# A fifth quad by seven products in gate/up pairs 1 to 8, with nine low parts a pair on GpSimd

## The reference

```python
    h = rmsnorm(x, norm_ffn[l])
    x = x + (jax.nn.silu(h @ w_gate[l]) * (h @ w_up[l])) @ w_down[l]
```

## Time and profile before

| | us |
|---|---|
| median of 3 runs | 2156.8 |
| lowest and highest of them | 2156.14 to 2157.34 |
| span of the profiled execution | 2155.3 |
| TensorE matmuls busy in it | 2144.2 |
| VectorE busy | 1771.7 |
| ScalarE busy | 1218.7 |
| GpSimd busy | 314.5 |

### The profile page before, as it was taken

One profiled execution on the slowest core, in us unless ns is written; L12 is line 12 of the kernel. 1 busy time (PEld: TensorE's weight loads), 2 busy tenths in 40 slices (PEclk: granted clock), 3 DMA queues, 4 the chain that ended last, 5 costly groups with the idle time before them and its releaser, 6 DMA issues.

```text
span 2155.3 us, 27924 instructions
## 1 busy us (share of the span) xinstructions
PE 2144.2 (99%) x10397; PEld 1794.4 (83%) x10397; DVE 1771.7 (82%) x2143; ACT 1218.7 (57%) x1714; POOL 314.5 (15%) x310
## 2 busy tenths in 40 slices
PE   9999999999999999999999999999999999999998
PEld 7888888888888888888888888888888888888886
DVE  5776676899899988999866666768998998988997
ACT  6454455666566555556554555546665665655564
POOL 0031120211221110000001211201112112100010
PEclk9999999999999999999999999999999999999999
DMA  9654445777777776767766444557777777756685
GB/s 349 203 183 176 176 157 189 212 218 223 246 217 229 227 229 205 227 216 221 246 200 217 171 161 157 176 194 212 218 229 232 219 222 244 221 198 219 219 240 181
DMA packets 152872, 456.81 MB, mean 212 GB/s; under 512 B 17440, under 2 KB 18080, under 8 KB 152352
## 3 DMA queue, kind: packets, MB, share of 16 engines
q1 hardware_dynamic: 132624, 416.41, 55.5%
q0 software_dynamic: 18816, 35.66, 9.8%
q10 hardware_dynamic: 1296, 2.94, 0.4%
HBM read 448.65 MB, written 2.10 MB: 209 GB/s over the span
## 4 chain that ended last, share of the span: by engine, by line
PE 97%; DVE 1%; ACT 1%; DMA 1%; POOL 0%; issue 0%; ACTq 0%; SPq 0%; DVEq 0%
PE bank L1861 16%; PE bank L1863 16%; PE bank L1862 16%; PE bank L1835 14%; PE bank L1875 9%; PE bank L1874 9%; PE bank L1873 9%; PE bank L1838 7%; PE bank L2039 1%; PE bank L1998 1%; PE bank L2021 1%; PE bank L1977 0%; DMA raw<-w_gu_dram 0%; POOL o_rms L675 0%; DVE wlo L1191 0%; PE bank L2007 0%
## 5 line engine op out<-in xcount | busy, mean ns | idle before, releaser
L761 ACT ACTIVATE whi<-raw 128x1024 fp32r<-128x1024 f32 x540 | 553.9, 1056 | 195.2 <-PE bank L1863 137.4
L1184 DVE TENSOR_TENSOR wlo<-raw,whi 128x1024 fp32r<-128x1024 f32 x504 | 606.9, 1229 | 65.9 <-ACT whi L761 64.9
L767 ACT ACTIVATE whi<-raw 128x1024 fp32r<-128x1024 f32 x480 | 430.0, 944 | 241.7 <-DVE raw L1206 139.6
L1191 DVE TENSOR_TENSOR wlo<-raw,whi 128x1024 fp32r<-128x1024 f32 x480 | 501.0, 1084 | 49.7 <-ACT whi L767 46.4
L1835 PE MATMUL bank<-xg,whi 128*128 128x512 f32 x1280 | 406.9, 399 | 1.0 <-DVE wlo L1440 1.0
L1861 PE MATMUL bank<-whi,xg 128*128 128x512 f32 x864 | 339.3, 393 | 0.5 <-DVE wlo L1184 0.5
L1863 PE MATMUL bank<-whi,xg 128*128 128x512 f32 x864 | 336.7, 390 | 0.0
L1862 PE MATMUL bank<-wlo,xg 128*128 128x512 f32 x864 | 336.5, 389 | 0.0
L1838 PEld LDWEIGHTS bank<-xg,wlo 128*128 128x128 f32 x1280 | 240.5, 188 | 56.9
L1838 PE MATMUL bank<-xg,wlo 128*128 128x256 f32 x1280 | 252.0, 278 | 0.0
L1835 PEld LDWEIGHTS bank<-xg,whi 128*128 128x128 f32 x1280 | 195.0, 189 | 3.3 <-DVE xg L1434 1.4
(11 more groups left out here) (161 smaller groups left out, 3050.7 us busy)
## 6 DMA issues: line engine op xcount, KB each, us to landing
raw<-w_gu_dram SPq DMA_DIRECT2D x268, 512.0 KB, 4.9
raw<-w_in_dram SPq DMA_DIRECT2D x188, 512.0 KB, 4.5
raw<-w_down_dram SPq DMA_DIRECT2D x140, 512.0 KB, 5.4
raw<-w_gu_dram SPq DMA_DIRECT2D x168, 256.0 KB, 4.2
raw<-w_out_dram SPq DMA_DIRECT2D x64, 512.0 KB, 4.4
raw<-w_gu_dram POOLq DMA_DIRECT2D x84, 256.0 KB, 5.7
raw<-w_down_dram SPq DMA_DIRECT2D x72, 256.0 KB, 4.7
raw<-w_down_dram POOLq DMA_DIRECT2D x36, 256.0 KB, 6.1
```

Source lines behind the costliest of these rows:

```text
L761: act.activation(whi[:, blk.slot(k)], raw[:, slot, half * UNIT_KT:(half + 1) * UNIT_KT, :], ACT.Copy).then_inc(hi_ready, 1)
L767: act.activation(whi[:, quad.slot(n), 0:tiles.stop - tiles.start], raw[:, quad.raw(), tiles, :], ACT.Copy).then_inc(hi_ready, 1)
L1184: dve.tensor_tensor(wlo[:, blk.slot(k)], raw[:, slot, half * UNIT_KT:(half + 1) * UNIT_KT, :], lo_bits(whi[:, blk.slot(k)]), ALU.subtract) ...
L1191: dve.tensor_tensor(wlo[:, quad.slot(n), into], raw[:, quad.raw(), tiles, :], lo_bits(whi[:, quad.slot(n), into]), ALU.subtract).then_inc( ...
```

## The change

- `GU_SEVENS` goes from 4 to 5: pairs 1 to 8 (`GU_FIVES`) do units 0 to 4 as quads and units 5 to 7 plainly, in a new order (`gu_five` on each engine). Pair 9 keeps four quads. Pair 0 does too, and in it the token-side forms of the fifth quad are made, by VectorE and ScalarE.
- In these eight pairs GpSimd makes nine low parts: of both units 5, both units 6 and the right unit 7, and the last part (two tiles) of quads 0 to 3. VectorE keeps the low parts of left unit 7, all first parts, the other second parts and all sums. In pair 0 GpSimd makes three low parts (right 5, left 6, right 7). It has no wait for a sum copy ahead of these.
- The three tiles of a quad's first parts are split by one operation on ScalarE and one on VectorE instead of two each, in every gate/up pair but the last.
- The high and low parts lie in ten tiles, placed by lists (`GU_FIVE_TILES` and others) instead of five slots in turn.
- Two more places for raw weights lie where `resid` is. ScalarE stores `resid` to DRAM in pair 0 (waiting for its squares), SP waits for the store ahead of pair 1's loads, loads it back ahead of pair 10's, and VectorE's fold of the first down pair waits for it.
- `sum_out` of a pair moves on ScalarE from its end to behind the first unit of the next pair.

```diff
-NSPLIT = 5
+NRAW_GU = NRAW + 2
+SPLIT_TILES = 10
...
-GU_SEVENS = 4
+GU_SEVENS = 5
...
-GU_FOURS = range(1, NGU // 2 - 1)
+GU_FIVE_ORDER = [("left", 5), ("right", 5), ("first", 0), ("first", 1), ("left", 6), ("second", 0), ("first", 2),
+                 ("right", 6), ("second", 1), ("first", 3), ("second", 2), ("first", 4), ("second", 3), ("second", 4),
+                 ("left", 7), ("right", 7)]
+GU_FIVE_TILES = [8, 6, 3, 0, 8, 6, 3, 0, 8, 5, 3, 0, 8, 6, 3, 0, 8, 6, 2, 4, 0]
+GU_FIVES = range(1, NGU // 2 - 2)
+GU_FOUR = NGU // 2 - 2
...
+    raw_gu = at("raw_gu", [P, NRAW_GU - NRAW, LOAD_KT, COLS], F32, resid_at)
+    resid_kept = nc.dram_tensor("resid_kept", (DEPTH, P, QT, DM), F32, kind="Internal").ap()
...
             for blk in plan.blocks[2:]:
+                if isinstance(blk, Pair) and blk.name == "gu" and blk.i == GU_FIVES[0]:
+                    sp.wait_ge(resid_out, 16 * (blk.layer + 1))
...
+                    sp.dma_start(resid[:], resid_kept[blk.layer]).then_inc(resid_back, 16)
...
+                for p in GU_FIVES:
+                    pair, later = (plan.pairs[layer, "gu", n] for n in (p, p + 1))
+                    left, right = pair.blocks
+                    split(left, 5)
+                    split(right, 5)
+                    add_b(pair.quads[2])
+                    split(left, 6)
+                    split_last(pair.quads[0])
+                    add_b(pair.quads[3])
+                    split(right, 6)
+                    split_last(pair.quads[1])
+                    add_b(pair.quads[4])
+                    split_last(pair.quads[2])
+                    split_last(pair.quads[3])
+                    add_b(later.quads[0])
+                    if later.five:
+                        add_b(later.quads[1])
+                    split(right, 7)
...
+                act.wait_ge(squared, (ffn + 1) * QT * NCH)
+                act.dma_start(resid_kept[layer], resid[:]).then_inc(resid_out, 16)
...
+            def gu_five(pair, prior):
+
+                q = [pair.quads[k] for k in range(GU_SEVENS)]
+                layer, before = prior.layer, [b.i for b in prior.blocks]
+                gates_ups(prior, 0, 1)
+                gates_ups(prior, 1, 0)
+                gates_ups(prior, 1, 1)
+                hidden_products(layer, before[0], 0)
+                hidden_products(layer, before[0], 1)
+                first_parts(q[0])
+                hidden_products(layer, before[1], 0)
+                hidden_products(layer, before[1], 1)
+                hidden_low(layer, before[0])
+                first_parts(q[1])
+                sums_of(q[0])
+                hidden_low(layer, before[1])
+                second_part(q[0])
+                sums_of(q[1])
+                first_parts(q[2])
+                second_part(q[1])
+                sums_of(q[2])
+                first_parts(q[3])
+                second_part(q[2])
+                sums_of(q[3])
+                first_parts(q[4])
+                sums_of(q[4])
+                second_part(q[3])
+                second_parts(q[4])
+                split(pair.blocks[0], 7, 8)
+                gu_fold(pair)
+                gates_ups(pair, 0, 0)
```

More of the change, by code:

```diff
@@ L196, in __init__ @@
                 q.added = plan.places[q.raw()]
-            if part in ("first", "second"):
+                q.joint = self.five or self.fours
+                q.split = [plan.split_unit(q.loads, t) for t in ((3,) if q.joint else (2, 1))]
+            elif part == "second":
                 q = self.quads[k]
-                q.split += [plan.split_unit(q.loads), plan.split_unit(q.loads)]
+                q.split += [plan.split_unit(q.loads, 2), plan.split_unit(q.loads, 2, by_pool=self.five and k in POOL_SECONDS)]
             else:
-                plan.unit(blocks[part == "right"], k, by_pool=self.fours and not self.first and k == POOL_UNIT)
+                plan.unit(blocks[part == "right"], k, by_pool=self.five and (part, k) != ("left", 7) or self.first and (part, k) in POOL_FIRST
+                          or self.fours and not self.first and k == POOL_UNIT)
         self.sums_taken = plan.taken[max(q.split[-1] for q in self.quads.values())][1]
@@ L268, in __init__, with split_unit @@
                         self.blocks.append(pair)
[L270 removed]
+    def split_unit(self, loads, tiles, block=None, last=False, by_pool=False):
         if last:
@@ L276, in split_unit @@
         n = len(self.taken) - 1
+        taken = tiles + tiles % 2 if tiles < 3 else tiles
+        if self.given:
+            self.next_tile = self.given.pop(0)
+        elif self.next_tile + taken > SPLIT_TILES:
+            self.next_tile = 0
+        span = slice(self.next_tile, self.next_tile + tiles)
+        self.span.append(span)
+        self.next_tile += taken
+        held = max(self.tile_held[span])
+        self.after.append(held if held >= 0 else None)
+        self.tile_held[span] = [n] * tiles
         for load in loads:
-            load.last = n
+            load.last["pool" if by_pool else "dve"] = n
         if by_pool:
@@ L918, in gu_rest @@
                 second_parts(q2)
+                if pair.first:
+                    form_high(pair.layer, "gu", GU_BATCHES - 1)
                 split(right, 6, 7)
@@ L1329, in gu_rest @@
                 other_sums(q1)
-                split(right, 5, 6)
+                if not pair.first:
+                    split(right, 5, 6)
                 second_parts(q1)
@@ L1334, in gu_rest @@
                 other_sums(q2)
-                split(left, 6, 7)
+                if pair.first:
+                    form_sums(pair.layer, "gu", GU_BATCHES - 1)
+                else:
+                    split(left, 6, 7)
                 second_parts(q2)
@@ L2067, in gu_four, with gu_five @@
                 gu_rest(pair)
+            def gu_five(pair):
+                left, right = pair.blocks
+                q = [pair.quads[k] for k in range(GU_SEVENS)]
+                plain(left, 5)
+                turn_hidden(pair.layer, 2 * pair.i - 2)
+                plain(right, 5)
+                turn_hidden(pair.layer, 2 * pair.i - 1)
+                first_products(q[0])
+                first_products(q[1])
+                plain(left, 6)
+                second_products(q[0])
+                first_products(q[2])
+                plain(right, 6)
+                second_products(q[1])
+                first_products(q[3])
+                second_products(q[2])
+                first_products(q[4])
+                second_products(q[3])
+                second_products(q[4])
+                plain(left, 7)
+                plain(right, 7)
             def gu_two(pair):
```

285 lines of the change are left out of this document (183 added, 102 removed).

## The result

The changed kernel takes 2369.8 us (median of four runs, 2368.7 to 2370.78), the kernel before 2157.07 us beside it (2156.14 to 2158.44). The ratio is 1.0988, 95% interval 1.0972 to 1.1003: slower by 213 us. The prediction said slower, 2288 us, with a range that ended at 2359.

A forecast was written before the change was run, and what follows sets the result against it. TensorE was taken as the bound (97% of the chain). VectorE's 33.1 + 6 x 2.21 + 3.6 us of waits gave 50.0 us a pair against 41.75, +131 us over 16 pairs: 2288 us, range 2210 to 2359.

The forecast's parts named there:

- the cause: Pairs 1 to 8: VectorE and GpSimd take strict turns when both want SBUF operands; neither runs beside the other.
- six collisions of nine: Of GpSimd's nine low parts a pair, both units 6 and the last parts of quads 0 to 3 block VectorE.
- their price: Each collision of a GpSimd low part with VectorE's SBUF work costs VectorE 2.21 us.
- the free edits: Residual's store taken as 0, at most 5 us a layer; its return 0; fifth adding transfer one more 0.86 us issue.
- pair 0: Three low parts fewer, fifth quad's forms and two collisions more for VectorE: taken as 0, at most 3 us a layer.
- VectorE's own work: VectorE's operations in a new pair, unblocked: 33.1 us, 5 us less than in the kernel before.
- 3.6 us of waits as today: VectorE's waits in each of pairs 1 to 8 stay as in the kernel before, 3.6 us a pair.
- a rival of 0.10: TensorE's new gaps could lower its clock; half speed for a fifth of a pair's matmuls would use its 9 us slack.
- TensorE stayed the bound: GpSimd's low parts find VectorE's PSUM work and waits, or VectorE gets in between: 2146 us in all, chance 0.08.
- good packing: Turns, but VectorE's waits fall beside GpSimd's work: 45.1 to 47 us a pair, 2210 to 2240 us, chance 0.15.
- eight collisions: Upper bound: eight of GpSimd's nine low parts block VectorE, 54.4 us a pair, +202 us.
- The last rival: Late-freed buffers make ScalarE wait: nine collisions, twice the waits, 60 us a pair, 2450 us; or lower TensorE clock; chance 0.10.

The follow-up runs named there:

- the write-only kernel: The changed kernel with GpSimd writing zeros in place of its gate/up low parts, reading no SBUF, those parts left out of the result: 2149.6 us.
- the copies: The changed kernel with GpSimd copying the high part in place of each low part, one SBUF operand read instead of two, low parts left out: 2204.39 us.
- the run with the clock kept: The changed kernel with TensorE adding products with zeros, 18 ahead of quad 2's first products and 10 ahead of quad 3's second products: 2329.81 us.

## Why the prediction was right in kind and wrong in size

**Right: the cause.** The two engines take turns at SBUF operands; the write-only kernel shows that the loss goes when GpSimd does not read, and the copies that a read of the same length brings part of it back.

**Right: six collisions of nine, and their price.** The six that collide are the very ones that the prediction names, in all eight pairs of the window. 2.21 us each was taken from the rows on GpSimd; 12.9 / 6 = 2.15 us was measured.

**Right: the free edits.** Parking the residual, the tile lists, SP's new wait and the fifth adding transfer cost 3.7 us together, net. **Nearly right: pair 0.** It was taken as 0, at most 3 us a layer; the first fold of layer 0 comes 3.7 us later than before (426.61 against 422.89), and at 424.45 where GpSimd only writes. In all 6.3 us of the loss lie outside the 16 pairs.

**Slightly low: VectorE's own work.** 33.1 us was taken, 34.19 is what it does unblocked. I priced a first sum at 0.60 us, the step between operations that don't need one another. The other sums need the first sum: from 564.15 to 564.94 the step is 0.79 us in the write-only kernel, 0.68 us of work and a gap of 0.11. Five of them are 0.4 of the 1.1 us; their gaps, 0.5 us a pair, count among the waits. The other 0.7 us was not broken down.

**Wrong: the term "3.6 us of waits as today".** It measured 7.65. Of the 4.05 us more, the run with the clock kept takes off 2.7, of which 1.6 ahead of the fold. The prediction named this mechanism, but only in a rival of 0.10, and priced it at nothing as long as TensorE had 9 us of slack a pair, up to half speed for a fifth of its matmuls; here 14 of 177 at half speed cost a pair 2.62 us. That is the step that failed: slack was counted over the whole pair, while the slow matmuls stand right behind a gap and ahead of the sum copy on which the fold waits, where there is none. What they delay, VectorE waits for, and the next low part comes later still. Of the remaining 1.4 us, 0.5 are the gaps behind the first sums. The last 0.9 is argued from rows and not isolated: when the last late low part is done at 638.14, TensorE has 24 matmuls to do, 5.4 us at full pace, and then ScalarE copies, while VectorE has only three operations left, 3.5 us. Today it has one more there, right 7, which the change gave to GpSimd. Where VectorE keeps right 7 and the rest, as with none, its waits are 1.44 us in all.

The sum with what was measured: 34.19 + 12.9 + 7.65 = 54.75 us a pair, 4.7 us over the forecast's 50.0; 16 pairs of it are 76 us, and with 6.3 us outside them the span of 2286.7 becomes 2369.

**The rivals.** With the fifth quad, TensorE stayed the bound only where GpSimd wrote its nine parts without reading SBUF. Times of 2210 to 2240 us did not come by good packing of nine parts; they took fewer parts on GpSimd (three, 2220 us; none, 2217). The range ended where eight collisions end, with no room for a longer wait on top of six. The last rival, which lies above it, had the waits doubled, as they were, but for nine collisions and 60 us a pair.

## What to carry to other kernels

Before work is moved from VectorE to GpSimd, count who reads SBUF beside whom: here a low part on GpSimd cost VectorE 1.43 us, more than the 1.05 us of making it itself. In these runs such work was free, or nearly so, only where it wrote without reading, or lay beside VectorE's PSUM operations or waits; that place has to be held by a wait, since it moves when VectorE gets faster. When a forecast opens gaps in TensorE, price the slow matmuls behind each gap as part of the path, not against the slack of the whole stage.

## What the runs showed that was not expected

- Fourteen matmuls a pair at half clock, 8% of 177, were worth 40 us, 1.7% of the kernel; 28 products with zeros in the gaps bought that back.
- GpSimd's writes cost VectorE's sums nothing: 0.68 and 1.23 us beside them, as unblocked.
- Two GpSimd operations of half the length hurt less than one: 2323 against 2370 us, though both read the same columns.
- Two parts more on GpSimd (five against three) left VectorE's busy time where it was and cost 57 us all the same, in waits: busy time alone does not show what a collision costs when what it delays is the next engine's start.
